# Output copy ahead of the rounding tiles, and VectorE's output sum and low parts ahead of the maximum, in an attention schedule

## The reference

```python
def attend(q, k, v, scale, mask=None, sink=None):
    s = jnp.einsum('bqhgd,bkhd->bhgqk', q.astype(jnp.float32), k.astype(jnp.float32)) * scale
    ...
        p = jax.nn.softmax(s, axis=-1)
    o = jnp.einsum('bhgqk,bkhd->bqhgd', p, v.astype(jnp.float32))
    return o.astype(v.dtype)
...
    o_m = dense_latent_attention(q_m, k_m, v_m, kc_m, vc_m, MLA_SCALE)
    o_s = window_latent_attention(q_s, k_s, v_s, kc_s, vc_s, sink, SWA_SCALE)
    o_a = dense_latent_attention(q_a, k_a, v_a, kc_a, vc_a, AX_SCALE)
    x = x + gate * merge_branches(o_m, o_s, o_a, z_m, z_s, z_a, g, lw)
```

## Time and profile before

| what | value |
| --- | --- |
| three executions, median (lowest to highest) | 1783.66 us (1782.36 to 1784.66) |
| profiled execution, span from the first to the last instruction | 1785.1 us |
| PE busy | 1711.1 us, 96% |
| VectorE busy | 1084.0 us, 61% |
| ScalarE busy | 1049.3 us, 59% |
| GpSimd busy | 528.0 us, 30% |
| PE waited for low parts of probabilities before `pv` | 21.2 us, 15 times |
| PE waited for the output sum before `pv` | 9.0 us, 12 times |
| VectorE waited for scores before the maximum | 166.2 us, 111 times |

### The profile page before, as it was taken

One profiled execution on the slowest core, in us unless ns is written; L12 is line 12 of the kernel. 1 busy time (PEld: TensorE's weight loads), 2 busy tenths in 40 slices (PEclk: granted clock), 3 DMA queues, 4 the chain that ended last, 5 costly groups with the idle time before them and its releaser, 6 DMA issues.

```text
span 1785.1 us, 27001 instructions
## 1 busy us (share of the span) xinstructions
PE 1711.1 (96%) x10554; PEld 1498.7 (84%) x10554; DVE 1084.0 (61%) x2185; ACT 1049.3 (59%) x1921; POOL 528.0 (30%) x300
## 2 busy tenths in 40 slices
PE   7999999999999999999999999999999999999997
PEld 3777888889989889899889996788888887888787
DVE  5543776765565566665775655477775756565634
ACT  3433778766666777666321253577776677786322
POOL 1523123222232212212322353322333432332442
PEclk9997999999999999999999999899999999999999
DMA  9111102111121111111644331111212221212642
GB/s 326 40 37 28 26 24 55 27 42 48 42 60 43 47 37 36 42 48 36 201 153 166 118 97 49 40 34 37 60 48 66 72 64 44 60 49 65 200 142 95
DMA packets 178527, 129.53 MB, mean 73 GB/s; under 512 B 21661, under 2 KB 167647, under 8 KB 178400
## 3 DMA queue, kind: packets, MB, share of 16 engines
q1 hardware_dynamic: 174242, 115.37, 22.7%
q10 hardware_dynamic: 2878, 8.24, 1.3%
q0 software_dynamic: 1280, 4.20, 0.7%
HBM read 123.58 MB, written 4.19 MB: 72 GB/s over the span
## 4 chain that ended last, share of the span: by engine, by line
PE 76%; DVE 10%; ACT 7%; issue 3%; POOL 2%; DMA 1%; SPq 0%; DVEq 0%; ACTq 0%; POOLq 0%
PE acc L1357 56%; PE wide L1415 6%; PE ptp L1435 6%; PE pv L1448 4%; PE pv L1449 3%; DVE nmax L1991 2%; ACT e L1682 2%; DVE pt L2016 1%; DMA w_raw<-in_ada_w 1%; POOL h_lo L1844 1%; DVE k_m L1552 1%; ACT w_hi L1600 1%; DVE k_s L1552 1%; DVE q_s L1552 1%; POOL w_lo L1806 1%
## 5 line engine op out<-in xcount | busy, mean ns | idle before, releaser
L1806 POOL TENSOR_TENSOR w_lo<-w_raw,w_hi 128x1024 fp32r<-128x1024 f32 (+2 forms) x192 | 392.0, 2045 | 1085.0 <-ACT w_hi L1600 1084.8
L1357 PE MATMUL acc<-h_hi,w_hi 128*128 128x512 f32 (+2 forms) x1320 | 463.3, 352 | 10.3 <-DVE cq_lo L1554 3.9
L1357 PE MATMUL acc<-h_hi,w_lo 128*128 128x512 f32 (+2 forms) x1320 | 462.0, 351 | 0.0
L1357 PE MATMUL acc<-h_lo,w_hi 128*128 128x512 f32 (+2 forms) x1320 | 457.7, 350 | 0.3 <-POOL h_lo L1844 0.3
L1991 DVE TENSOR_REDUCE nmax<-wide 128x1 f32<-128x768 f32 (+3 forms) x240 | 189.6, 790 | 167.9 <-PE wide L1415 166.2
L1357 PEld LDWEIGHTS acc<-h_hi,w_hi 128*128 128x128 f32 (+1 forms) x1320 | 248.4, 188 | 50.1 <-issue 7.9
L1697 ACT ACTIVATE pt<-ptp 128x512 fp32r<-128x512 f32 (+3 forms) x312 | 165.8, 563 | 210.4 <-PE ptp L1435 208.6
L1357 PEld LDWEIGHTS acc<-h_hi,w_lo 128*128 128x128 f32 (+1 forms) x1320 | 248.2, 188 | 33.4
L1357 PEld LDWEIGHTS acc<-h_lo,w_hi 128*128 128x128 f32 (+1 forms) x1320 | 246.1, 188 | 34.2 <-POOL h_lo L1844 0.5
L1689 ACT ACTIVATE e<-e,einv 128x768 f32<-128x768 f32 (+3 forms) x240 | 193.5, 806 | 70.2 <-DVE einv L2008 69.8
L2016 DVE TENSOR_TENSOR pt<-ptp,pt 128x512 fp32r<-128x512 f32 (+3 forms) x312 | 191.8, 640 | 43.9 <-ACT pt L1697 43.7
(11 more groups left out here) (216 smaller groups left out, 3103.1 us busy)
## 6 DMA issues: line engine op xcount, KB each, us to landing
w_raw<-in_w_in SPq DMA_DIRECT2D x102, 512.0 KB, 3.9
w_raw<-in_ada_w SPq DMA_DIRECT2D x48, 512.0 KB, 5.3
w_raw<-in_w_out SPq DMA_DIRECT2D x16, 512.0 KB, 4.2
w_raw<-in_w_in SPq DMA_DIRECT2D x16, 256.0 KB, 3.3
w_raw<-in_w_o_mla SPq DMA_DIRECT2D x16, 256.0 KB, 2.8
w_raw<-in_w_o_swa SPq DMA_DIRECT2D x16, 256.0 KB, 2.8
w_raw<-in_w_o_ax SPq DMA_DIRECT2D x16, 256.0 KB, 2.9
w_raw<-in_mla_w_uq SPq DMA_DIRECT2D x16, 144.0 KB, 2.4
```

What stands on the lines that cost most here:

```text
L1357: ins = nc.tensor.matmul(dst, lhs, rhs, start=first, stop=last)
L1806: nc.gpsimd.tensor_tensor(w_lo[s][:, 0:k], w_raw[s][:, 0:k], f(w_hi[s][:, 0:k]), ALU.subtract).then_inc(w_lo_ready, 1)
```

## The change

The diff reorders events of one turn. `OC` moves from behind the maximum to the front of `T`, and `O` and `TL` move from behind `X` to the place ahead of it, with `O` before `TL`. No instruction is added or removed, and the rows of PE, POOL and SP are in the order they had. All lines below the edit have numbers that are smaller by one.

```diff
                 PV(t)
                 if t["last"]:
                     turned = t["pa"]
+            if turned:
+                emit("OC", pa=turned)
             if coming and coming[0]["units"][-1]["n"] <= i + first - 2:
                 waiting += coming.pop(0)["tiles"]
             valued, waiting = waiting[:2], waiting[2:]
@@ -469,15 +471,12 @@
                 SB(u)
             if 0 < i <= len(units):
                 emit("N", u=units[i - 1])
+            if turned:
+                O(turned)
+            for t in valued:
+                emit("TL", t=t)
             if u:
                 X(u)
-            if turned:
-                emit("OC", pa=turned)
-            for t in valued:
-                emit("TL", t=t)
-            if turned:
-                O(turned)
-            if u:
                 M(u)
                 if u is u["pa"]["units"][-1]:
                     coming.append(u["pa"])
```

## The result

The kernel after the change takes 1885.5 us in the median (1880.2 to 1889.9, four executions), the kernel before 1783.6 us. The ratio is 1.0577, with a 95% interval from 1.0549 to 1.0604: 102 us are lost, where 11.5 us had been forecast, and the time lies far outside the range of 1777 to 1806 us. The direction was right, the size was not.

What follows compares the result with a forecast made beforehand. PE, busy 96% of the span, was taken as the bound, so only its waits could change. Terms 10.5 + 1 - 1 + 1 + 0 = +11.5 us on 1783.7 us gave 1795 us; 8-in-10 range 1777 to 1806 us.

Steps and rivals of the forecast that it cites:

- the deciding number: Slack per unit: start of PE's next scores less end of the exponentials; PE loses what the exponentials' delay exceeds it by.
- layer 0's `mla`: First stage: four heads at 2.3 us and three losing 1.3 us together, +10.5 us; half of that or +16 us possible.
- layer 1's `mla`: Small gains at one-tile turns, 0.2 us lost some ten times at pass ends: +1 us, ends -3 and +5.
- the shift: How much later exponentials come: up to 1.56 us (two tiles 2.2 us), less VectorE's wait for scores and the copy's 0.4 us.
- `swa` and `ax`: Slacks of 1.6 to 2.9 us cover shifts of 0.5 to 1.5 us: -1 us, ends -4 and +1.
- The turn that was worked out: Units 19 and 20 in layer 0's `mla`: PE 1.1 us later at the first, the head 2.3 us later.
- The step into `o_t`: Output product held by GpSimd, now ahead of the exponentials: +1 us, bounds 0 and +12 us.
- The clock: PE's lower clock behind long waits at `pv`, four stretches in the attention: 0, ends -6.8 and +7 us.
- the wait of `wide` for `e`: Sign: PE's scores wait 15 us or more for exponentials, mostly between 180 and 390 us; under 5 us, the slack rule fails.
- VectorE's wait for scores: Sign: VectorE's wait for scores before the maximum falls far below 166 us.
- the wait before `pv`: Sign: PE's wait at `pv` for low parts and output sum falls from 30.2 us to under 18 us.
- Much slower: the shift goes round: Rival: later exponentials delay reads, high and low parts, and the output meets GpSimd more: +24 us, 1808 us, chance 0.15.

Runs made afterwards that it cites:

- the wait alone: Against the kernel before, same order of work, but VectorE waits for ScalarE's high part ahead of the maximum: 1808.05 us, ratio 1.0142.
- the ladder: Runs lined up from copy early; maximum, sum, low parts, product (0.9952) to the kernel after (1.0577); steps: waits 27, length 22, product's length 24, GpSimd's holds 38 us.
- the sum in PSUM: Kernel after in its order, but the output sum is written back to `pv` in PSUM and the product reads it there: 1851.5 us, ratio 1.0364.
- the extra work: Kernel before plus 312 unused maxima over SBUF columns on VectorE: 1844.5 us ahead of the maximum (1.0336), 1805.2 us behind the output (1.0125).

## Why the prediction was wrong

**The direction and the deciding number were right, in part.** PE loses where the exponentials come later than its next scores could start. In the kernel after PE waits for exponentials 53 times, and its next scores start less than 0.1 us behind their end in 26 of 48 turns of layer 0's `mla` (before: 6), in 14 of 32 of layer 1's `mla` and in 11 of 32 of its `swa` (before: none in either). But the run with the wait alone lost 24.5 us with that wait unchanged at 1.2 us. The waits that grew there are those at `pv`, where the prediction expected only gain.

**The step that failed: the shift, and the slack set against it.** The prediction took as shift what VectorE has to do (0.68 us per tile, 0.88 us per pass) and set it against slacks of 1.6 to 2.9 us in `swa` and `ax`, with the result "Nothing on PE's path". That left out a wait: a low part ahead of the maximum can't start before ScalarE's high part, and that stands behind PE's transposes, or behind the exponentials of the turn before and the reads that follow. In the kernel after, of the 71 waits for it 42 lead back to the exponentials without a gap and 29 to the transposes. In before VectorE waited 43.7 us for high parts, 26 times for 312 tiles, when it came to them after the maximum; the prediction doesn't look at that wait. Moved alone it costs 24.5 us. But the larger error is in what had been counted: on the ladder the omitted wait is 27 us, the lengths, priced at 10.5 + 1 - 1 = 10.5 us, are up to 46 us, and the holds, priced at 1 us, are some 38 us.

**Layer 0's `mla`: 10.5 us forecast, 35.3 us lost.** The turn that was worked out (0.7 to 2.3 us per head) let the delay end with the head. In a ring it needn't: a later exponential makes the next reads, the next low part and the next maximum later. In the profiled executions this stage lost 11.0 us with the wait alone, 12.9 with the low parts alone, 17.2 with the output alone, and of the 35.3 us the sum in PSUM gave back 8.6 (35.3 less 26.7).

**Layer 1's `mla`: +1 us forecast, 20.3 us lost. `swa` and `ax`: -1 us forecast, 47.7 us lost** (4.3 + 20.4 + 7.0 + 16.0). This is the largest miss. The slacks of the trace of before were treated as a reserve that the shift may eat, one turn at a time. They were no such reserve for the whole order. But the wait alone didn't spend them everywhere: its run lost nothing in `swa` (-0.5 and -0.3 us), and 4.5 and 4.3 us in `ax`.

**The step into `o_t`: +1 us forecast with 12 us as upper end, some 38 us lost.** It was assumed that product and GpSimd meet by chance, at most 36 times with 0.65 us each, and that slack eats half. They met 46 times, with 0.82 us each (37.6 / 46), and nothing was eaten. The number of meetings goes with the product's place: 46 here, 36 with the output alone ahead, 19 right behind the maximum and the sum, and 6 to 10 in the nine other orders with the sum in SBUF, before's included. Why so many meet is argued here and not tested, since no run moved GpSimd's work alone: they may no longer be independent. GpSimd's low parts of weights start when ScalarE's high part of the weights is done, which is fill work behind the exponentials, and the product now starts right behind ScalarE's copy, at the head of the next turn. All 46 products overlap an instruction of GpSimd, and end 0.27 to 0.29 us after its end; in 32 that is the low parts of weights, in 14 a step of a rotation, which hangs on VectorE and not on ScalarE. One more, with GpSimd's instruction from 278.20 to 280.60:

```profile
279.02 1.86 DVE L2028 SCALAR_TENSOR_TENSOR o_t<-o_half,o_t 64x256 f32<-64x256 f32 x1
```
```profile
278.20 2.40 POOL L1805 TENSOR_TENSOR w_lo<-w_raw,w_hi 128x1024 fp32r<-128x1024 f32 x1 [1.46 <-ACT w_hi L1599]
```

The Trainium skill, page SBUF — State Buffer, section "Who interferes with whom", says that a VectorE instruction with two SBUF inputs contends with a GpSimd instruction that reads SBUF, and one with at most one SBUF input does not, outside its two-port modes. The runs agree on both halves: with the second input in PSUM none of 120 products was over 0.43 us. The rule had been cited in the prediction, and then its price was set low.

**The clock: 0 with ends of 7 us, 27 us between the first and the last maximum.** The prediction was right that the lower level comes with waits, but there were more of them: 7 stretches at the lower level lie there in before, with 41.6 us of idle PE, and 17 in after, with 96.4 us. Ahead of the first maximum before's profiled execution was the one with the lower clock, so that over the whole span only 18 us are seen. Two stretches of the kernel after (PEclk is the eighth value):

```profile
210.00:220.00 10.00, 9.90 (x62) 8.23 (x61) 8.41 (x18) 6.37 (x15) 4.42 (x4) 1.00 0.23 56
220.00:230.00 10.00, 6.48 (x20) 4.86 (x19) 7.07 (x11) 4.79 (x9) 2.16 (x3) 0.66 0.01 2
```

In the second, PE is busy 6.48 us and is granted 0.66 of full speed, which is a mixture of the two levels. That time is contained in each step of the ladder.

**What had been named as signs.** Foretold and seen: the wait of `wide` for `e` (15 us or more; 43.9 us), VectorE's wait for scores far below 166 us (4.0 us), durations over 0.5 us in L2028 other than eight (46). Foretold and not seen: the wait before `pv` under 18 us (31.4 us), the wait for exponentials mostly between 180 and 390 us (15.3 of 43.9 us), layer 0's `swa` within 2 us (4.3 us).

**The rival that named the mechanism.** "Much slower: the shift goes round" names the ring, the reads behind the exponentials and the product that meets GpSimd, and gives them 24 us and a chance of 0.15; its 1808 us are 77 us short. It was priced by taking the upper end of terms that had been worked out without the ring. A mechanism that feeds back was not priced by that.

**What stays open.** Which of the two rings, over ScalarE's queue or over PE, costs how much of the wait's 24.5 to 27 us. The 22 us that the extra work costs at the end of the turn are explained in part: from the first maximum to the last PE idles 11.5 us more than in before, 8.5 us of it before `pv` for low parts (29.7 against 21.2 us), and 8.5 us more go to the lower clock. The stretch ahead of the first maximum, which no run changes, differs by up to 9 us between the profiled executions with its granted clock; the intervals cover this only as far as it changes from execution to execution. The four steps of the ladder hold for this path; on another path they may share out differently, since low parts alone (38) and output alone (32) give 70, and together 102 us.

## What to carry to other kernels

Before an instruction is put ahead of the head of a chain (here the maximum), write down what it waits for, and on which engine's queue that stands. If it leads back to the chain's own last turn, engines that ran side by side now run in series, and slack read from the old trace is no reserve. Keep ahead of the maximum as little as can be: even work that waits for nothing cost 60 us there, and 22 us at the end of the turn. Split a step if only its first half frees a buffer: here the sum ahead of the low parts and the product last won 0.5%, where the whole step ahead of the maximum lost. Where GpSimd works beside it, VectorE's product of two SBUF operands belongs where nobody waits behind it, or one of the operands belongs in PSUM.

## What the runs showed of the hardware

VectorE's product with both inputs in SBUF was held for up to 1.95 us (2.37 less 0.42) by GpSimd, until 0.28 us after GpSimd's instruction, whether that was a low part of weights or a rotation; the unused maxima over one SBUF operand never were (266 to 690 ns in 2 x 312, their lengths those of 128 to 512 columns), though 54 and 38 of them lay wholly within an instruction of GpSimd. That the one is held and the other is not is as the Trainium skill, page SBUF — State Buffer, section "Who interferes with whom", says. Not expected was how much the meetings depend on the product's place in the turn: 46 of 120, 36 and 19 in three orders and 6 to 10 in the others, with GpSimd busy 30% or 28% of the span in before and after. A semaphore wait with no work moved cost 24.5 us, 1.4% of the kernel.
